# Expert rows scaled at their copy and added into the residual by adding gathers, in a float32 two-block layer on one core

## The chip, the cores and the metric

One Trainium2 chip, one of its cores. The metric is the device time of one execution of the whole program, in microseconds. The kernel before has a median of 2668.73 us over 3 runs (2668.01 to 2673.38). All times below are of one profiled execution of it unless the text says otherwise, counted from the start of its span.

## The reference

The program computes two blocks on 512 tokens of width 1024, in float32. The first block is a retention and pooling mixer, a mixture of experts and a gated side input; the second a state-space mixer, a convolution mixer and two feed-forward layers. The change lies in the mixture of experts and in what follows it directly:

```python
def moe(hn, router_w, router_b, w_gu, b_gu, w_down, b_down):
    logits = xt @ router_w + router_b
    top_vals, top_idx = lax.top_k(logits, TOP_K)        # 4 of 32
    gates = jax.nn.softmax(top_vals, axis=-1)
    ...
    gu = lax.ragged_dot(xs, w_gu, group_sizes) + b_gu[sorted_e]
    act = (up + 1.0) * (gate * jax.nn.sigmoid(SWIGLU_ALPHA * gate))
    y = lax.ragged_dot(act, w_down, group_sizes) + b_down[sorted_e]
    y = y * gates.reshape(-1)[order][:, None]
    return jnp.zeros_like(xt).at[tok].add(y)

h = h + moe(rms_norm(h, norm_moe_w), ...)
gate = jax.nn.sigmoid(rms_norm(h, norm_ple_w) @ ple_gate_w)
h = h + gate * (p @ ple_proj_w)
```

## The kernel before, in words

Every engine has its own program, written out by hand, and semaphores tie them together; there is no scheduler. So the order of an engine's instructions is the order of the code.

**Router (about 260 to 300 us).** VectorE picks four experts per token (`choose`), gives each of the 2048 (token, expert) pairs a tile and a row in it (tiles of 128 rows; expert e owns tile e, further tiles are numbered from 32), and builds one-hot matrices `row_hot` (pair to row) and `tile_token`. TensorE multiplies them (L2374): the product is, per tile, which token stands in each row. VectorE then makes the gates (`gate_table`, L1704), copies the token ids to integers (L1735) and lets GpSimd gather the first tile's tokens (L771). `extra_tables` (L1715) makes the indices by which rows are fetched at the end.

**Experts (300 to 1440 us).** For e = 0 to 31: 8 weight tiles up, 4 down, each split by ScalarE (`slot_hi`, L995) and VectorE (`slot_lo`, L1760) into two parts, for three products on TensorE (L2417). `store_y` (L1017) copies the 128 rows of expert e - 1 or e - 2 from PSUM to `y_sb` and stores them to `y_dram`, unscaled. GpSimd gathers the tokens of the next tile. With the inputs used here no expert has more than 128 tokens, so the code under `If(extra > 0)` is not run.

**Combine (1440 to 1545 us).** After the last store GpSimd issues 16 gathers (`take`, L787), four per group of 128 tokens, into 16 buffers `got`. VectorE adds the down biases, which TensorE has multiplied by the gates (L2504, L1845), and then for each token group i four rows times gate (`combine`, L1853, 16 instructions on L1856). Each group is squared and summed on ScalarE (`moe_square`), its inverse root taken on VectorE (`ple_rstd`), transposed on TensorE (`token_columns`), and multiplied by `ple_w_sb` (`ple_gate`, L2519, two halves per group) whose rows ScalarE has scaled before (L1114). `ple_product` (L2527) is the side input times its weights; `ple_add` on VectorE joins the two. Between these VectorE places steps for the next stage: `c_power` (three instructions, L1849 to L1851) eight times, `turn_angles` and `reduce_turns`. ScalarE's sine block (L1194 on) waits for the last of these, and the second block's first transposes wait for it. SP loads `m_t` for the next stage (8 transfers) once `s_got_used` is 3.

The order of TensorE around the change is:

```python
pe.wait_ge(s_prep_dve, 5)
pe.wait_ge(s_ple_in, 48)
columns_of(p_rows, 2)
...
ple_product(0)
token_columns(0)
for i in range(NT):
    ple_gate(i, 0)
    if i:
        ple_product(i)
    if i + 1 < NT:
        token_columns(i + 1)
    ple_gate(i, 1)
```

## Time and profile before

| | us |
|---|---|
| median of 3 runs | 2668.73 |
| the profiled execution, its own time | 2666.62 |
| its span | 2664.9 |
| TensorE busy (matmul) | 2579.0 |
| VectorE busy | 1947.5 |
| ScalarE busy | 1355.8 |
| GpSimd busy | 198.2 |

The span runs from the first to the last instruction in the trace; the execution's own time has 1.7 us around it. A busy share is an average over stages with different limits, so each stretch has to be read by itself. Rows of the timeline give start, duration, engine, line, operation, output and inputs, and in brackets how long the engine stood idle before and what released it. DMA rows give the time from the issue on the engine's queue to the last byte's semaphore.

### The profile page before, as it was taken

The page shows a single profiled execution, that of the slowest core. Times are in us where ns is not written, and L with a number is a line of the kernel's source. Part 1 is how long each engine was busy: PE and PEld are TensorE (multiplying, and loading weights), DVE is VectorE, ACT ScalarE, POOL GpSimd, SP SyncE. Part 2 cuts the span into 40 slices and gives each one's busy share as a digit, 9 for nine tenths or more (in the row PEclk, how much of TensorE's full clock was granted, in tenths as well). Part 3 has the DMA queues.
Part 4 walks back from the last instruction along what each step waited for, and adds up shares of the span by engine and source line. Part 5 has one row for each costly group of instructions (what it writes and reads, how often), then busy time and mean ns, then how long its engine had stood idle before and what let it go on. Part 6 is the DMA issues. An engine that isn't in the chain of part 4 may idle for free.

```text
span 2664.9 us, 34816 instructions
## 1 busy us (share of the span) xinstructions
PE 2579.0 (97%) x12452; PEld 2113.6 (79%) x12452; DVE 1947.5 (73%) x1892; ACT 1355.8 (51%) x1366; POOL 198.2 (7%) x297
## 2 busy tenths in 40 slices
PE   9999899999999999999998978999999999999998
PEld 7777788888888888888885467888888887888886
DVE  7968899999999999999998986566633444543422
ACT  5232777777777777777775343322222222322222
POOL 2241100000000000000002000011100000000000
PEclk9999999999999999999998998999999999999999
DMA  9734899999999999999996922277643632133432
GB/s 343 280 137 126 356 362 410 384 388 385 387 383 385 390 383 384 387 386 386 385 362 237 161 76 77 59 224 225 188 113 87 156 95 56 48 95 100 108 94 75
DMA packets 351280, 643.89 MB, mean 242 GB/s; under 512 B 27056, under 2 KB 220464, under 8 KB 350192
## 3 DMA queue, kind: packets, MB, share of 16 engines
q1 hardware_dynamic: 327840, 542.88, 59.5%
q0 software_dynamic: 17872, 78.13, 8.3%
q10 hardware_dynamic: 5504, 22.02, 2.0%
q8 instruction: 41, 0.67, 0.1%
q14 instruction: 23, 0.19, 0.0%
HBM read 616.82 MB, written 26.16 MB: 241 GB/s over the span
## 4 chain that ended last, share of the span: by engine, by line
PE 71%; issue 15%; DVE 10%; DMA 2%; ACT 2%; POOL 0%; ACTq 0%; POOLq 0%; DVEq 0%; SPq 0%
PE bank L2417 39%; PE bank L2664 8%; PE bank L2670 8%; PE bank L2665 8%; PE bank L2393 1%; PE bank L2405 1%; DVE cb L1433 1%; PE bank L2400 1%; DMA ring<-in_w_in 1%; PE bank L2227 1%; DVE rows L1856 1%; PE bank L2229 1%; PE bank L2228 1%; DVE ring L2004 0%; DMA m_w_dram<-work 0%
## 5 line engine op out<-in xcount | busy, mean ns | idle before, releaser
L1760 DVE TENSOR_TENSOR slot_lo<-ring,slot_hi 128x2048 fp32r<-128x2048 f32 x384 | 863.7, 2285 | 68.2 <-ACT slot_hi L995 67.8
L995 ACT ACTIVATE slot_hi<-ring 128x2048 fp32r<-128x2048 f32 x384 | 736.5, 1921 | 252.9 <-PE bank L2417 226.6
L2417 PE MATMUL bank<-slot_hi,xs_hi 128*128 128x512 f32 x1024 | 316.8, 391 | 0.0
L2417 PE MATMUL bank<-slot_hi,xs_lo 128*128 128x512 f32 x1024 | 315.7, 389 | 0.0
L2664 PE MATMUL bank<-h_hi,fin_hi 128*128 128x512 f32 x704 | 275.1, 391 | 0.0
L2665 PE MATMUL bank<-h_hi,fin_lo 128*128 128x512 f32 x704 | 274.1, 389 | 0.0
L2417 PE MATMUL bank<-slot_lo,xs_hi 128*128 128x512 f32 x1024 | 274.1, 389 | 0.0
L2417 PEld LDWEIGHTS bank<-slot_hi,xs_lo 128*128 128x128 f32 x1024 | 192.4, 188 | 40.8
L2417 PEld LDWEIGHTS bank<-slot_hi,xs_hi 128*128 128x128 f32 x1024 | 192.5, 188 | 40.2
L2417 PEld LDWEIGHTS bank<-slot_lo,xs_hi 128*128 128x128 f32 x1024 | 192.2, 188 | 40.2
L1255 ACT ACTIVATE fin_hi<-rows 128x1024 fp32r<-128x1024 f32 x88 | 88.2, 1052 | 215.5 <-DMA rows<-in_w_ffn_in 215.5
L2025 DVE TENSOR_TENSOR fin_lo<-rows,fin_hi 128x1024 fp32r<-128x1024 f32 x88 | 103.7, 1221 | 115.2 <-ACT fin_hi L1255 113.1
L2670 PE MATMUL bank<-h_lo,fin_hi 128*128 128x512 f32 x704 | 166.7, 389 | 0.0
L2417 PE MATMUL bank<-slot_hi,act_hi 128*128 128x512 f32 x512 | 161.1, 396 | 2.7 <-DVE act_lo L1769 2.7
L2417 PE MATMUL bank<-slot_hi,act_lo 128*128 128x512 f32 x512 | 158.2, 390 | 0.0
L2664 PEld LDWEIGHTS bank<-h_hi,fin_hi 128*128 128x128 f32 x704 | 132.2, 188 | 28.4 <-issue 1.0
L2670 PEld LDWEIGHTS bank<-h_lo,fin_hi 128*128 128x128 f32 x704 | 132.2, 188 | 27.4
L2665 PEld LDWEIGHTS bank<-h_hi,fin_lo 128*128 128x128 f32 x704 | 132.2, 188 | 27.2
L2417 PE MATMUL bank<-slot_lo,act_hi 128*128 128x512 f32 x512 | 137.7, 391 | 0.0
L2664 PE MATMUL bank<-f_hi,fout_hi 128*128 128x512 f32 x352 | 137.6, 391 | 0.0
L2665 PE MATMUL bank<-f_hi,fout_lo 128*128 128x512 f32 x352 | 137.0, 389 | 0.0
L1300 ACT ACTIVATE ring<-bank 128x512 f32<-128x512 f32 x60 | 35.8, 597 | 195.2 <-PE bank L2670 195.2
(448 smaller groups left out, 4060.0 us busy)
## 6 DMA issues: line engine op xcount, KB each, us to landing
ring<-in_expert_w_gate_up SPq DMA_DIRECT2D x256, 1024.0 KB, 7.1
ring<-in_expert_w_down SPq DMA_DIRECT2D x128, 1024.0 KB, 6.6
rows<-in_w_ffn_in SPq DMA_DIRECT2D x88, 512.0 KB, 4.9
work<-in_w_ada POOLq DMA_DIRECT2D x64, 384.0 KB, 3.8
y_dram<-cb ACTq DMA_DIRECT2D x32, 512.0 KB, 6.9
rows<-in_w_ada POOLq DMA_DIRECT2D x35, 384.0 KB, 5.9
work<-in_w_ffn_out SPq DMA_DIRECT2D x8, 1408.0 KB, 7.0
rows<-in_w_ffn_out SPq DMA_DIRECT2D x8, 1408.0 KB, 6.8
```

Of the source, the lines that this page charges most:

```text
L995: act.activation(hi_of(e, j), slot[q], ACT.Copy).then_inc(s_slot_hi, 1)
L1255: act.activation(split[n][0][b][:, v], raw[:, v], ACT.Copy).then_inc(s_w_hi, 1)
L1300: act.activation(sig_sb[b], ps[3 * b + bank][:], func).then_inc(s_lin_sig, 1)
L1433: return stt(acc, w, cact[:, k:k + 1], acc, ALU.mult, ALU.add)
L1760: tt(slot_lo[:, q], slot[q], whole(hi_of(e, j)), ALU.subtract).then_inc(s_slot_lo, 1)
L1856: ins = stt(rows[:, i, :], got[n], weights[:, n:n + 1], rows[:, i, :], ALU.mult, ALU.add)
L2025: tt(split[n][1][at][:, v], buf[at][:, v], whole(split[n][0][b][:, v]), ALU.subtract).then_inc(s_w_lo, 1)
L2227: mm(ps[i][:], mix_hi[:, k, tokens], w_hi[:, k, :], start=(k == 0), stop=False)
L2417: last = mm(ps[banks + n], x[:, k, :], (lo if lower else hi)[:, k, 512 * n:512 * (n + 1)], start=(begins and lower == 0 and k == 0 and x i ...
L2664: mm(ps[3 * b + v][:], w_hi[b][:, v, k, :], x_hi[:, k, :], start=(k == 0), stop=False)
L2665: mm(ps[3 * b + v][:], lo[:, v, k, :], x_hi[:, k, :], start=False, stop=False)
L2670: last = mm(ps[3 * b + v][:], w_hi[b][:, v, k, :], x_lo[:, k, :], start=False, stop=(k == depth[n] - 1))
```

## The change

1. The gate goes to the row where it is computed. `gate_table` also builds `tile_gate` (one-hot over 48 tiles times gate), 16 small products on TensorE give `slot_gate`, the gate of every row of every tile, and the copy of an expert's rows out of PSUM is scaled by it (`scaled_y`; one more 128x1 copy per tile brings the gate to a fixed place).
2. The 16 gathers add into `rows` in the DMA (`compute_op=ALU.add`). Adds into the same group must follow each other, so each waits for the one before it on that group: groups 0 and 1 alternately, k = 0 to 3, then groups 2 and 3. They start when tile 30 has been stored. VectorE's 16 multiply-adds go.
3. The last expert's rows aren't stored: 8 one-hot products (`last_hot`) add them in PSUM beside the down bias, and `y_dram`'s last tile holds zeros (`zero_rows`). `last_rows` replaces `add_down_bias`.
4. The ids are copied before `gate_table`; `extra_tables` moves between two weight splits of expert 0.
5. The norm weights are applied to `h_cols` (8 copies of 128x128 per group) and no longer to the 16 pieces of `ple_w_sb`.
6. The orders around it: below and in the diff. SP's `m_t` loads no longer wait for `s_got_used` 3.

```diff
+ROW_PAIR = (3, 0, 2, 1)
...
@@ SP
-            sp.wait_ge(s_slot_done, extra * 12 + 12 * E - 4)
+            sp.wait_ge(s_sig_ready, extra * 2 + 2 * E)
...
             sp.wait_ge(s_k_out, 16 * (CH + 1))
-            sp.wait_ge(s_got_used, 3)
@@ GpSimd
+            def add_rows(source, index, i, k, done):
+                n = index + TOPK * i + k
+                pool.indirect_dma_start(
+                    out=rows[:, i, :], out_offset=None, in_=source, compute_op=ALU.add,
+                    in_offset=bass.IndirectOffsetOnAxis(ap=smi[:, n:n + 1].bitcast(U32), axis=0)).then_inc(done, 16)
...
+            pool.wait_ge(s_zero_rows, 16)
+            pool.wait_ge(s_y_stored, 16 * E)
+            for first in (0, 2):
+                for k in range(TOPK):
+                    for i in (first, first + 1):
+                        if k:
+                            pool.wait_ge(s_got_in[i], 16 * k)
+                        add_rows(y_dram, 20, i, k, s_got_in[i])
...
-            take(y_dram, 20, s_got_in)
@@ ScalarE
+            def scaled_y(tile, done, stored, home=y_sb):
+                act.wait_ge(s_slot_gate, 2)
+                act.wait_ge(s_y_sb, tile * 2 + 1)
+                act.activation(gate_col, slot_gate[:, bass.ds(tile, 1)], ACT.Copy).then_inc(s_gate_col, 1)
+                act.wait_ge(s_slot_done, done)
+                act.wait_ge(s_y_stored, stored)
+                act.wait_ge(s_gate_col, tile + 1)
+                for n in range(2):
+                    act.activation(home[:, 512 * n:512 * (n + 1)], ps[4 + n], ACT.Copy, scale=gate_col).then_inc(s_y_sb, 1)
...
+            act.dma_start(zero_rows, whole(pick[:].rearrange("p n t -> p (n t)")).unsqueeze(1).broadcast_to([P, 4, 2 * P])).then_inc(s_zero_rows, 16)
...
-            act.wait_ge(s_ple_in, 48)
-            for n in range(2):
-                for k in range(KD):
-                    act.activation(ple_w_sb[n][:, k, :], ple_w_sb[n][:, k, :], ACT.Copy,
-                                   scale=vcol("norm_ple_w", k)).then_inc(s_prep_act, 1)
@@ VectorE
+                step(tt(tile_gate, iota[:, 0:TILES].unsqueeze(1).broadcast_to(picked),
+                        pick_t.unsqueeze(2).broadcast_to(picked), ALU.is_equal))
+                tt(tile_gate, tile_gate, flat_gates, ALU.mult).then_inc(s_slot_gate, 1)
...
-            def add_down_bias(i):
+            def last_rows(i):
                 dve.wait_ge(s_gates_ps, i + 2)
-                tt(rows[:, i, :], rows[:, i, :], pairs[i][:], ALU.add).then_inc(s_prep_dve, 1)
+                dve.wait_ge(s_got_in[i], 16 * TOPK)
+                tt(rows[:, i, :], rows[:, i, :], pairs[ROW_PAIR[i]][:], ALU.add).then_inc(s_got_used, 1)
...
+            for v in range(2):
                 c_power(v)
+            last_rows(0)
+            last_rows(1)
+            c_power(2)
+            ple_rstd(0, 1)
+            last_rows(2)
+            last_rows(3)
+            ple_rstd(1, 2)
+            ple_rstd(2, 4)
+            c_power(3)
+            c_power(4)
             ple_add(0)
@@ TensorE
+            for n in range(NT * TOPK):
+                last = mm(ps[5][:, 0:TILES], row_hot[:, n, :], tile_gate[:, n, :], start=(n == 0), stop=(n == NT * TOPK - 1))
+            last.then_inc(s_ids_ps, 1)
...
+                    mm(bank, gates_t[n][:, P * i:P * (i + 1)], down_bias[n], start=True, stop=False)
+                    last = mm(bank, last_hot[:, i, :], y_sb[:, 512 * n:512 * (n + 1)], start=False, stop=True)
...
+                if i < 2:
+                    pe.wait_ge(s_got_used, 2 + 2 * i)
...
+                else:
+                    pe.wait_ge(s_side_in, 80)
+                    pe.wait_ge(s_got_used, 3)
```

How the order stands at the three places that matter. First VectorE at the router's end, before (L1707 to L1713 are the gate table, L1735 the ids):

```order
L1707 TENSOR_REDUCE sm<-sm 128x4 [waits norm_in,gate_e,dve_step]
L1708 RECIPROCAL sm<-sm 128x4 [waits dve_step]
L1709 TENSOR_TENSOR sm<-sm 128x16 [waits dve_step]
L1710 TENSOR_TENSOR sm<-sm,work 128x16 [waits dve_step]
L1711 TENSOR_TENSOR sm<-sm 128x16 [waits dve_step]
L1712 TENSOR_TENSOR work<-work,sm 128x512 [waits dve_step]
L1713 TENSOR_REDUCE work<-work 128x128 [waits dve_step]
L1735 CAST smi<-bank 128x48 [waits ids_ps]
```

and now (L1755 the ids, L1733 and L1735 the new `tile_gate`):

```order
L1755 CAST smi<-bank 128x48 [waits ids_ps,dve_step]
L1757 COPY sm<-bank 128x1 [waits dve_step]
L1728 TENSOR_REDUCE sm<-sm 128x4 [waits norm_in,gate_e,dve_step]
L1729 RECIPROCAL sm<-sm 128x4 [waits dve_step]
L1730 TENSOR_TENSOR sm<-sm 128x16 [waits dve_step]
L1733 TENSOR_TENSOR work<-const,work 128x768 [waits k_ps,dve_step]
L1735 TENSOR_TENSOR work<-work,sm 128x768 [waits dve_step]
L1737 TENSOR_TENSOR work<-work,sm 128x512 [waits slot_gate]
L1738 TENSOR_REDUCE work<-work 128x128 [waits dve_step]
```

The ids moved from behind the gate table to its front, past a wait for a DMA (`norm_in`). Second, GpSimd's gathers now (before: 16 without a wait between them but one for `gates_ps` after the eighth):

```order
L788 DMA rows<-y_dram,smi 128x1024 [waits y_stored,zero_rows]
L788 DMA rows<-y_dram,smi 128x1024
L788 DMA rows<-y_dram,smi 128x1024 [waits got_in0]
L788 DMA rows<-y_dram,smi 128x1024 [waits got_in1]
L788 DMA rows<-y_dram,smi 128x1024 [waits got_in0]
L788 DMA rows<-y_dram,smi 128x1024 [waits got_in1]
L788 DMA rows<-y_dram,smi 128x1024 [waits got_in0]
L788 DMA rows<-y_dram,smi 128x1024 [waits got_in1]
L788 DMA rows<-y_dram,smi 128x1024 x2
L788 DMA rows<-y_dram,smi 128x1024 [waits got_in2]
```

Five more rows of this kind, waiting for `got_in3` and `got_in2` in turn, follow. Third, TensorE now, from the last expert on (L2522 and L2523 bias and one-hot products, L2539 `ple_gate`, L2550 `ple_product`):

```order
L2523 MATMUL bank<-cb,work 128x512
L2206 MATMUL bank<-const,rows 128x128 [waits cols_taken,got_used]
L2206 MATMUL bank<-const,rows 128x128 x3
L2206 MATMUL bank<-const,rows 128x128 [waits cols_taken]
L2206 MATMUL bank<-const,rows 128x128 x3
L2539 MATMUL bank<-ring,ca 128x512 [waits got_used,cols_taken]
L2539 MATMUL bank<-ring,ca 128x512 x7
L2550 MATMUL bank<-work,ca 128x512 [waits got_used,side_in]
L2550 MATMUL bank<-work,ca 128x512 x3
L2206 MATMUL bank<-const,rows 128x128 [waits cols_taken,got_used]
```

`ple_product(0)`, which stood before the first `ple_gate` and waited for no gather, stands behind it and waits for `s_got_used` 3, that is for token group 2.

## Rows read from the trace of the kernel before

**Rows 1.** Expert loop: whom ScalarE waited for (us, times, longest)

```profile
ACT slot_hi L995 <- PE bank L2417: 224.3, 308, 1.3
```

**Rows 2.** Timeline of TensorE at the router's end: start, us, engine, line, operation

```profile
281.62 3.91 PE L2374 MATMUL bank<-cb,work 128*128 128x48 f32 x32 [0.67 <-ACT cb L975]
...
290.51 1.13 PE L2383 MATMUL bank<-const 128*128 128x256 f32 x4 [0.69 <-ACT nat L840]
296.99 1.94 PE L2393 MATMUL bank<-const,work 128*128 128x128 f32 x8 [5.35 <-DMA work<-hn_dram,smi]
```

**Rows 3.** Timeline of GpSimd there, the first gather of tokens

```profile
290.10 3.02 POOL L771 DMA_INDIRECT work<-hn_dram,smi  x1 [15.41 <-DVEq L1736]
```

**Rows 4.** Timeline of VectorE at the router's end

```profile
286.81 0.17 DVE L1707 TENSOR_REDUCE sm<-sm 128x4 f32<-128x16 f32 x1 [3.16 <-DMA m_w_dram<-work]
...
289.56 0.20 DVE L1735 CAST smi<-bank 128x48 int32<-128x48 f32 x1
```

**Rows 5.** Chain of waits that ended last, 1440 to 1545: start, us, what

```profile
1441.21 6.50 DMA y_dram<-cb
...
1465.49 1.29 DVE rows L1856
```

**Rows 6.** Timeline of TensorE after the last expert

```profile
1456.20 5.21 PE L2527 MATMUL bank<-work,ca 128*128 128x512 f32 x8 [0.78 <-ACT ca L840]
...
1467.23 9.94 PE L2519 MATMUL bank<-ring,ca 128*128 128x512 f32 x16 [1.18 <-ACT ca L840]
1477.01 1.04 PE L2197 MATMUL bank<-const,rows 128*128 128x128 f32 x8
1477.89 13.90 PE L2519 MATMUL bank<-ring,ca 128*128 128x512 f32 x32
1491.62 3.60 PE L2527 MATMUL bank<-work,ca 128*128 128x512 f32 x8
```

**Rows 7.** Timeline of VectorE, 1480 to 1525

```profile
1480.67 1.22 DVE L1849 TENSOR_TENSOR ring<-work,cb 128x1024 f32<-128x1024 f32 x1
...
1484.44 0.69 DVE L1876 TENSOR_TENSOR cb<-cb,bank 128x512 f32<-128x512 f32 x1
...
1487.10 5.24 DVE L1856 SCALAR_TENSOR_TENSOR rows<-nat,sm,rows 128x1024 f32<-128x1024 f32 x4
1493.55 0.17 DVE L1372 TENSOR_SCALAR sm<-sm 128x2 f32<-128x2 f32 x1 [1.22 <-ACT cb L845]
...
1496.11 1.22 DVE L1881 TENSOR_TENSOR nat<-rows,ca 128x1024 f32<-128x1024 f32 x1 [0.23 <-DVE sm L1367]
...
1508.72 0.38 DVE L1907 COPY sm<-par 64x32 f32<-64x32 f32 x2
...
1523.57 0.69 DVE L1876 TENSOR_TENSOR nat<-nat,bank 128x512 f32<-128x512 f32 x1 [0.22 <-DVE work L1382]
```

**Rows 8.** Timeline of ScalarE, 1424 to 1500

```profile
1424.89 0.35 ACTq L1023 DMA_DIRECT2D y_dram<-cb  x1
...
1443.95 9.91 ACT L1114 ACTIVATE ring<-ring,vec 128x512 f32<-128x512 f32 x16 [2.77 <-DMA ring<-in_ple_gate_w]
...
1484.96 0.69 ACT L1139 ACTIVATE cb<-bank,sm 128x512 f32<-128x512 f32 x1 [5.05 <-PE bank L2519]
1492.37 1.06 ACT L845 ACTIVATE cb<-rows 128x1024 f32<-128x1024 f32 x1 [6.73 <-DVE rows L1856]
```

**Rows 9.** Timeline of GpSimd: one of the sixteen issues

```profile
1452.25 0.94 POOL L791 DMA_INDIRECT ring<-y_dram,smi  x1 [0.30 <-issue]
```

**Rows 10.** Issue to landing: GpSimd's gathers of expert rows, L791

```profile
DMA to landing us min/median/max: 5.3/6.0/7.6
```

**Rows 11.** Issue to landing: GpSimd's gathers of tokens in the loop, L762

```profile
DMA to landing us min/median/max: 5.0/5.9/8.8
```

**Rows 12.** Stretches: us, busy PE, PEld, DVE, ACT, POOL, PEclk, DMA share, GB/s

```profile
1440.00:1444.00 4.00, 0.98 (x3) 0.50 (x4) 3.90 (x4) 1.13 (x3) 0.00 (x0) 0.78 1.05 400
1444.00:1448.00 4.00, 4.00 (x12) 1.69 (x10) 3.90 (x4) 4.00 (x7) 0.13 (x1) 0.50 0.51 203
```

More of the change, by code:

```diff
@@ L393, in program @@
         s_y_stored = sem("y_stored")
-        s_more_zero = sem("more_zero")
+        s_zero_rows = sem("zero_rows")
+        s_slot_gate = sem("slot_gate")
+        s_gate_col = sem("gate_col")
         s_ct_ps = sem("ct_ps")
@@ L784, in _ @@
                     next_tile(n + E)
-            def take(source, index, done):
-                for n in range(NT * TOPK):
-                    if n == 2 * TOPK:
-                        pool.wait_ge(s_gates_ps, NT + 1)
-                    pool.indirect_dma_start(
-                        out=got[n], out_offset=None, in_=source,
-                        in_offset=bass.IndirectOffsetOnAxis(ap=smi[:, index + n:index + n + 1].bitcast(U32), axis=0),
-                    ).then_inc(done[n // TOPK], 16)
-            pool.wait_ge(s_y_stored, extra * 16 + 16 * (E + 1))
-            pool.wait_ge(s_xst_ready, extra * 2 + 2 * E + 2)
-            pool.tensor_tensor(smi[:, 130:131], smi[:, 52:53], smi[:, 52:53], ALU.add)
-            with pool.If(extra > 0):
-                take(y_more, 36, [s_more_in] * NT)
-                pool.wait_ge(s_more_used, NT)
-            take(y_dram, 20, s_got_in)
+                pool.wait_ge(s_y_stored, extra * 16 + 16 * E)
+                pool.tensor_tensor(smi[:, 130:131], smi[:, 52:53], smi[:, 52:53], ALU.add)
+                for i in range(NT):
+                    pool.wait_ge(s_got_in[i], 16 * TOPK)
+                for k in range(TOPK):
+                    for i in range(NT):
+                        if k or i:
+                            pool.wait_ge(s_more_in, 16 * (NT * k + i))
+                        add_rows(y_more, 36, i, k, s_more_in)
             def token_rstd(n):
@@ L1131, in token_columns @@
                 for r in range(2):
-                    column(h_cols[i % 2][:, 512 * r:512 * (r + 1)], first=6)
+                    n = rounds[0]
+                    rounds[0] += 1
+                    act.wait_ge(s_cols_ready, n + 1)
+                    for k in range(4 * r, 4 * r + 4):
+                        part = act.activation(h_cols[i % 2][:, P * k:P * (k + 1)], ps[6 + n % 2][:, P * (k % 4):P * (k % 4 + 1)],
+                                              ACT.Copy, scale=vcol("norm_ple_w", k))
+                    part.then_inc(s_cols_taken, 1)
             def ple_gate(i, n):
@@ L1698, in _ @@
             step(dve.tensor_copy(smi[:, 52:56], token))
-            step(ts(ext_e, pick_t, float(E), None, ALU.is_ge))
-            more, main = sm[:, 176:192], sm[:, 160:176]
             gate_rows = work[:, 8192:8192 + NT * E].rearrange("p (i e) -> p i e", i=NT)
@@ L1797, in _ @@
             split_low(0, 0)
-            extra_tables()
             tokens_low(0)
@@ L1802, in _ @@
                 split_low(0, j)
+                if j == 3:
+                    dve.wait_ge(s_ids_ps, 2)
+                    dve.tensor_copy(slot_gate, ps[5][:, 0:TILES]).then_inc(s_slot_gate, 1)
+                    extra_tables()
             swiglu(0, 0)
@@ L1824, in _ @@
                 low_ahead(E, j)
+            for i in range(NT):
+                step(ts(last_hot[:, i, :], iota, float(P * i), last_token, ALU.add, ALU.is_equal))
+            dve.sem_inc(s_prep_dve, 1)
             n0 = step.n
@@ L1851, in c_power @@
                 step(tt(m_c[:, :, v, :], m_c[:, :, v, :], s5_tb, ALU.add))
-            def combine(i, weights, done):
-                for k in range(TOPK):
-                    n = TOPK * i + k
-                    ins = stt(rows[:, i, :], got[n], weights[:, n:n + 1], rows[:, i, :], ALU.mult, ALU.add)
-                    if k < TOPK - 1:
-                        step(ins)
-                    else:
-                        ins.then_inc(done, 1)
-            def combine_main(i):
-                dve.wait_ge(s_got_in[i], 16 * TOPK)
-                combine(i, main, s_got_used)
             def ple_rstd(first, end):
```

118 lines of the change are left out of this document (48 added, 70 removed).

## The prediction

> **What bounds the kernel now.** I read the chain of waits first, then each engine's timeline in the two stretches that the change touches, then the landing times of the gathers. The expert loop (300 to 1440 us) is TensorE's: the split and the copies wait for it, ScalarE alone 224.3 us in 308 waits [rows 1]. So the change can gain or lose only at the router's end and between the last expert and the second block.
>
> At the router's end TensorE stands still for 5.35 us until the first gather of tokens lands at 296.99 [rows 2]. That gather is issued at 290.10 [rows 3], when VectorE has copied the ids at 289.56, behind a gate table that could begin only at 286.81 because of a DMA [rows 4]. The ids' product was done at 281.62 + 3.91 = 285.5 [rows 2].
>
> After the last expert the chain goes through the last store (6.50 us), the gathers, and then VectorE's multiply-adds [rows 5]. The reader is to see that from 1477.9 on TensorE and VectorE are both nearly full: TensorE's first product behind group 0, `ple_product(1)`, starts at 1491.62 without a gap [rows 6], and VectorE reaches `ple_add(2)`, which lets the sine block begin, at 1523.57 with 0.22 us idle [rows 7]. Whoever is late sets the end, and both hang on `ple_add(0)`.
>
> **The sum, part by part.**
>
> *Ids first.* They are copied at about 285.7 instead of 289.56, and the gather, whose issue to landing is 296.99 - 290.10 = 6.9 us, issued at about 286.1, lands at 293.0. But TensorE now first does 16 small products for `slot_gate`, of the same shape as the ids' (3.91 us). They wait for VectorE: 286.81, three small steps (0.6), two 768-wide steps of about 1.0 each (the 512-wide part of the gate table took less): 289.6. TensorE is free at 290.5, since the two keep-warm products of 1.13 us go [rows 2]. So it reaches the tokens at 290.5 + 3.9 = 294.4 instead of 296.99: **-2.6 us**. Bounds: 0, if the longer table is late, and -4.0, if only the gather counted. `extra_tables` (2.6 us now) goes between two splits of expert 0; this costs nothing as long as VectorE is ahead of TensorE there. The zero store is issued on ScalarE's queue before the tokens arrive and is waited for ten microseconds later.
>
> *In the loop.* Each tile gets one 128x1 copy on ScalarE, at most 0.3 us, and it stands ahead of the wait for the products. ScalarE waits 224.3 us for TensorE in the loop [rows 1], 32 copies are some 10: **0**. If that cover went, 10 us is the price.
>
> *Start of the adding gathers.* Tile 30's store is issued at 1424.89 [rows 8]; with the 6.50 of the last one [rows 5] it has landed at 1431.4, against 1447.9 before. GpSimd has nothing else then. That is 16 us earlier, and it is what the change is paid with.
>
> *Their length.* The old 16 were issued every 0.94 + 0.30 = 1.25 us [rows 9] and overlapped. Now each waits for the one before on its group. Issue to landing was 6.0 (5.3 to 7.6) [rows 10] and 5.9 (5.0 to 8.8) beside the weights' loads [rows 11]. An add must read the row as well as the source; 0.5 MB at 400 GB/s [rows 12] is 1.3 us, so I take 7.3 per round. No row shows an adding DMA: the ends are 5.0, the shortest plain one, and 8.8 + 1.3 = 10.1. Groups 0 and 1 alternate; group 2 begins two issues behind their fourth round. Group 2 has landed at 1431.4 + 7 x 7.3 + 2.5 = 1485.0, and `last_rows(2)` (1.2) ends at **1486.2**. Under the Trainium skill, page "Collectives: The Full Stack", section "The bandwidth ceiling: the fold count and why AG ≠ RS ≠ AR", a DMA that adds costs twice the source reads and nothing for the sum itself. By that rule the round would be about the same 7.3, and no run here shows it yet.
>
> *TensorE up to there.* The gate weights land at 1443.95 [rows 8], say 1446 with gathers beside them. Then the side input's columns (2.0, twice the 0.9 of eight transposes at full clock [rows 6]), 16 products of 128x512 (0.86 each at full clock from 13.9 / 16 [rows 6], 13.7 in all; 17 taken, because the granted clock is 0.50, 1.2 of 2.4 GHz, behind the pause at 1440 [rows 12]), transposes (1.0), eight copies on ScalarE (2), `ple_gate(0, 0)` (7.3): 1475.3. Bounds 1468.8 (all at full clock) and 1486. There it waits for 1486.2, because `ple_product(0)` needs group 2. **TensorE stands still for 11 us.**
>
> *From there to `ple_add(0)`.* Behind a pause the clock is halved: `ple_product` took 5.2 then and 3.6 later, `ple_gate` 9.94 against 6.9 [rows 6]. So 5.2 + 1.0 + 8.0 (clock back on the way) = 14.2 until `ple_gate(0, 1)` ends. ScalarE squares group 3 only behind that half's sigmoid: 0.7 + 1.2 [rows 8]. VectorE's order puts `ple_rstd(2, 4)` (2.6) and two `c_power` (3.8 each) before `ple_add(0)` (2.7) [rows 7]: 0.7 + 1.2 + 2.6 + 7.6 + 2.7 = 14.8 us, in which TensorE has only 7 us of work. `ple_add(0)` ends at 1486.2 + 14.2 + 14.8 = **1515.2**.
>
> *From `ple_add(0)` on* the order is the old one: `z_rows` 1.2, three `c_power` 11.3, `ple_add(1)` 2.7, `z_rows` 1.2, `turn_angles` and `reduce_turns` 1523.57 - 1508.72 = 14.9 [rows 7], together 31.3. To meet the old 1523.57 `ple_add(0)` would have to end at 1492.3; TensorE's own 1491.62 says the same. It ends **22.9 us later**. The 16 multiply-adds that VectorE sheds (4 x 5.24 = 21 us [rows 7]) turn into waiting, since VectorE stands at `last_rows(2)` and at `ple_rstd(2, 4)`. The 16 weight scalings (9.9 us [rows 8]) and the 13.7 us of new products also lie inside the wait.
>
> Sum: 22.9 - 2.6 = +20.3. The profiled execution's own time is 2666.6, so 2686.9; against the median of the runs, 2668.7, it is **2689 us**.
>
> **The rivals.**
>
> *B, gathers hidden behind TensorE.* If group 2 has landed by 1475 (a round under 5.8 us), TensorE doesn't pause: 1475.3 + 3.4 + 0.9 + 6.9 + 14.8 = 1501.3, +9.0 - 2.6 = +6.4: 2675. For it: 5.9 and 6.0 are medians under load. Against: the add reads more. By the Trainium skill, page "DMA: Bandwidth & Descriptors", section "Anatomy of one DMA — SWDGE (gpsimd) path", one such DMA takes 2.0 us plus its bytes at 436 GB/s, an estimate of 3.2 for 0.5 MB; by that rule B would hold. The trace disagrees: none of the 48 gathers took under 5.0.
>
> *C, gathers slowed by what they run beside.* Rounds of 10.1: group 2 at 1431.4 + 70.7 + 2.5 + 1.2 = 1505.8, `ple_add(0)` 1534.8, +39.9: 2709. For it: the gate weights load until 1444, and SP's eight `m_t` loads now start when group 1 is done, beside the gathers of groups 2 and 3. Against: beside the weights' loads the median stayed 5.9.
>
> *D, the other side: VectorE was the bound, and its 21 us come back.* The chain before does run through the multiply-adds. If gathers land by 1462 (a round under 3.9) and the square of group 3 doesn't hold VectorE, only TensorE's work is left: 1443.95 + 2.0 + 13.7 + 0.9 + 1.3 = 1461.9, then 6.9 + 3.4 + 0.9 + 13.8 = 1486.9 for `ple_product(1)` against 1491.6: -4.7 - 2.6 = -7.3: 2661. It decides once no gather is waited for. Against: eight dependent rounds can't fit, and the written order holds VectorE.
>
> *E, it cancels.* Gathers as in B and TensorE at its lower bound of 1468.8: 1468.8 + 11.2 + 14.8 = 1494.8, +2.5 - 2.6 = 0: 2669, also what a saving that nobody waits for would give.
>
> **How the numbers follow.** Forecast (serial gathers, a pause of TensorE) 0.48; B 0.17; C 0.16; D 0.09; E 0.10. A measurement of this kernel tells 0.2%, 5.3 us, from no change. Slower is forecast, B and C: 0.81; same E: 0.10; faster D: 0.09. The range leaves out D, half of E and the top of C (rounds above 10.7): 2668 to 2714. The forecast's own range, rounds of 6.5 to 8.3, is 2683 to 2696.
>
> **What would show it.** The first add issued near 1429 (the front gain shifts all by 2.6), rounds of about 7 us, in pairs; TensorE idle for some 10 us before `ple_product(0)` and for 5 to 8 before `ple_product(1)`, its granted clock at 0.5 behind each; VectorE idle before `last_rows(2)` and `ple_rstd(2, 4)`; TensorE's tokens at 294.4. I am wrong if adds overlap, if `ple_add(0)` ends before 1495, or if the front idle stays at 5 us.

## The result and the profile after

| | before | after |
|---|---|---|
| median of the runs, us | 2669.54 (2667.69 to 2673.38, 6 runs) | 2723.4 (2716.16 to 2730.3, 6 runs) |
| profiled execution, us | 2666.62 (span 2664.9) | 2725.22 (span 2723.5) |
| TensorE busy, us | 2579.0 | 2612.1 |
| VectorE busy, us | 1947.5 | 1928.5 |
| GpSimd busy, us | 198.2 | 208.1 |

The ratio is 1.0199, 95% interval 1.0186 to 1.0212: 2.0% slower, 53.9 us. I forecast 2689, slower, with a range of 2668 to 2714. The direction was right. The forecast loss, 20.3 us, was less than half of the measured one, and the time lies outside the range. Below, a token tile is the same as a token group: 128 of the 512 tokens.

In this execution the ids' product starts at 284.79 instead of 281.62, ahead of everything that the change touches. Why was not traced; in the profiled executions of the other runs it starts between 1.5 us earlier and 4.0 us later than before. So some 3 us of every shift below are not the change's, and starts of two runs can be compared only to a few us.

TensorE, timeline of after, the first product that each stretch waits for (columns: start and length in us, engine, line, operation, out<-in, shape, count, idle before it and what ended the idle time):

```profile
293.59 4.27 PE L2390 MATMUL bank<-work 128*128 128x48 f32 x32 [0.69 <-ACT nat L850]
297.66 1.93 PE L2405 MATMUL bank<-const,work 128*128 128x128 f32 x8
...
329.69 0.72 PE L2417 MATMUL bank<-bias_parts,pick 128*128 128x512 f32 x2 [3.65 <-DVE xs_lo L1799]
...
1453.25 1.97 PE L2206 MATMUL bank<-const,work 128*128 128x128 f32 x8 [10.39 <-DMA ring<-in_ple_gate_w]
1455.15 2.07 PE L2522 MATMUL bank<-work 32*128 32x512 f32 x2
1457.15 2.07 PE L2523 MATMUL bank<-cb,work 128*128 128x512 f32 x2
...
1490.36 7.13 PE L2539 MATMUL bank<-ring,ca 128*128 128x512 f32 x16 [1.82 <-ACT ca L1153]
1521.05 5.87 PE L2550 MATMUL bank<-work,ca 128*128 128x512 f32 x8 [23.56 <-DVE rows L1876]
...
1549.30 5.42 PE L2550 MATMUL bank<-work,ca 128*128 128x512 f32 x8 [7.77 <-DVE rows L1895]
```

The row at 1549.30 is `ple_product(1)`, which before started at 1491.62 [rows 6]: 57.7 us later, as the whole span is 58.6 longer. So the loss is whole by then, and nothing behind it adds. It is set by the gathers of tile 2, for which TensorE waits 23.56 us ahead of `ple_product(0)`, and by the 28.3 us from there to `ple_product(1)`, 7.77 of them a second wait. TensorE's own work ended at 1497.5. That lies inside the gathers' time here, but late: the sixteen row products (bias and one-hot) took 2.0 us each, so a shorter wait would soon have met them.

GpSimd, timeline of after, the sixteen adding gathers (the idle time before a row is the wait for the one before on the same tile):

```profile
1436.88 1.70 POOL L788 DMA_INDIRECT rows<-y_dram,smi  x1 [52.70 <-DMA y_dram<-cb]
1438.88 1.87 POOL L788 DMA_INDIRECT rows<-y_dram,smi  x1 [0.30 <-issue]
1447.16 2.49 POOL L788 DMA_INDIRECT rows<-y_dram,smi  x1 [6.41 <-DMA rows<-y_dram,smi]
...
1457.45 1.54 POOL L788 DMA_INDIRECT rows<-y_dram,smi  x1 [5.54 <-DMA rows<-y_dram,smi]
...
1464.34 1.56 POOL L788 DMA_INDIRECT rows<-y_dram,smi  x1 [1.87 <-DMA rows<-y_dram,smi]
...
1469.35 1.55 POOL L788 DMA_INDIRECT rows<-y_dram,smi  x1 [0.30 <-issue]
...
1476.22 2.40 POOL L788 DMA_INDIRECT rows<-y_dram,smi  x1 [3.46 <-DMA rows<-y_dram,smi]
...
1491.75 1.55 POOL L788 DMA_INDIRECT rows<-y_dram,smi  x1 [9.14 <-DMA rows<-y_dram,smi]
...
1505.25 1.55 POOL L788 DMA_INDIRECT rows<-y_dram,smi  x1 [8.34 <-DMA rows<-y_dram,smi]
```

Tile 0 issues at 1436.88, 1447.16, 1457.45 and 1464.34: rounds of 10.3, 10.3 and 6.9. Tile 2 issues at 1469.35, 1476.22, 1491.75 and 1505.25: 6.9, 15.5, 13.5. What changes between a round of 6.9 and the others stands on SyncE's queue (the eight loads together, from the start of the first issue to the end of the last), and what it costs on VectorE:

```profile
1475.22 46.23 SPq L527 DMA_DIRECT2D ring<-k_dram  x8
```

```profile
1470.68 1.22 DVE L1876 TENSOR_TENSOR rows<-rows,bank 128x1024 f32<-128x1024 f32 x1 [21.20 <-DMA rows<-y_dram,smi]
1473.58 1.22 DVE L1876 TENSOR_TENSOR rows<-rows,bank 128x1024 f32<-128x1024 f32 x1 [1.69 <-DMA rows<-y_dram,smi]
1519.69 1.22 DVE L1876 TENSOR_TENSOR rows<-rows,bank 128x1024 f32<-128x1024 f32 x1 [38.92 <-DMA rows<-y_dram,smi]
```

The `m_t` loads (`ring<-k_dram`) start at 1475.22, as soon as `last_rows(1)` lets them, and from then on the rounds are twice as long. In the kernel before they started at 1478.41, when the last gather had been issued 7.9 us before, at 1470.54. The first two rounds of tile 0 run beside the gate weights, which were issued 4.2 us later than before and land at 1453.25 instead of 1443.95 [rows 8].

### The profile page after: what moved, and what is told of

Its sections match the earlier page's. It is cut to its first block, busy times and chain, and to the rows that moved or that the text cites. A ratio compares the mean times of both kernels' runs of the same rounds, so it can differ in the third digit from the quotient of the medians.

```text
span 2723.5 us, 35024 instructions
## 1 busy us (share of the span) xinstructions
PE 2612.1 (96%) x12496; PEld 2126.4 (78%) x12496; DVE 1928.5 (71%) x1878; ACT 1359.1 (50%) x1406; POOL 208.1 (8%) x297
## 4 chain that ended last, share of the span: by engine, by line
PE 68%; issue 15%; DVE 10%; DMA 5%; ACT 2%; POOL 0%; SPq 0%; ACTq 0%; DVEq 0%; POOLq 0%
PE bank L2429 37%; PE bank L2684 7%; PE bank L2678 7%; PE bank L2679 7%; DMA rows<-y_dram,smi 3%; PE bank L2405 1%; DVE cb L1456 1%; PE bank L2417 1%; PE bank L2412 1%; DMA ring<-in_w_in 1%; DVE slot_lo L1783 1%; PE bank L2236 1%; PE bank L2237 1%; PE bank L2238 1%; DMA rows<-in_w_ffn_in 1%
## 5 line engine op out<-in xcount | busy, mean ns | idle before, releaser
L1005 ACT ACTIVATE slot_hi<-ring 128x2048 fp32r<-128x2048 f32 x384 | 733.0, 1918 | 245.1 <-PE bank L2429 218.9
```

The costliest lines, as they stand in the source:

```text
L1005: act.activation(hi_of(e, j), slot[q], ACT.Copy).then_inc(s_slot_hi, 1)
```

## The experiments

Two theories stood at first. **M**: the `m_t` loads, no longer held by `s_got_used` 3, slow the gathers of tiles 2 and 3. **A**: the adding itself is slow. Later runs took apart what stood behind each bound that a run removed. Unless said otherwise a start is that of the profiled execution.

### 1. The m_t loads behind the gathers

```diff
             sp.wait_ge(s_k_out, 16 * (CH + 1))
+            sp.wait_ge(s_got_used, NT)
             for v in range(CH):
                 load(m_t[...], ..., s_t_in)
```

> The changed kernel, but SP's eight m_t loads wait for all four token groups (s_got_used 4). Theory M: these loads stretch the adding rounds of groups 2 and 3 from 6.9 us (the two rounds at 1457 and 1469, with nothing beside them) to 13.5 to 15.5. Then the rounds go back to about 7, group 2 lands at 1469.4 + 4 x 7 = 1497 instead of 1519.6, and the time is about 2701. Rival N: two adding gathers in flight are slow of themselves; then nothing changes, 2723.

Measured: 2703.06 (2701.48 to 2704.25), ratio 1.0124 (1.0105 to 1.0142), so 20.3 us come back. TensorE's timeline of this kernel:

```profile
1453.12 1.97 PE L2207 MATMUL bank<-const,work 128*128 128x128 f32 x8 [11.83 <-DMA ring<-in_ple_gate_w]
...
1490.26 8.96 PE L2540 MATMUL bank<-ring,ca 128*128 128x512 f32 x16 [1.41 <-ACT ca L1154]
1499.06 3.60 PE L2551 MATMUL bank<-work,ca 128*128 128x512 f32 x8
...
1525.03 5.21 PE L2551 MATMUL bank<-work,ca 128*128 128x512 f32 x8 [7.77 <-DVE rows L1896]
```

and VectorE's:

```profile
1493.27 1.22 DVE L1877 TENSOR_TENSOR rows<-rows,bank 128x1024 f32<-128x1024 f32 x1 [14.94 <-DMA rows<-y_dram,smi]
```

Tile 2 lands at 1493.3 instead of 1519.7, its rounds are 7.6, 7.6 and 6.6, and TensorE no longer waits ahead of `ple_product(0)`: its own work, which reaches it at 1499.06, has become the bound. M holds and is worth 20 us. The gathers by themselves would have let it start at 1494.5, so this bound lies only 4.6 us behind theirs. The loads' own lateness costs nothing: `m_t` is read only behind the x columns, the first of which start at 1573.75 in this kernel.

### 2. Gathers that copy instead of add

```diff
-                    out=rows[:, i, :], out_offset=None, in_=source, compute_op=ALU.add,
+                    out=rows[:, i, :], out_offset=None, in_=source,
```

This leaves out the adding: of each token only the last gathered row remains, without the residual. The chain of waits is that of after.

> The changed kernel, its 16 gathers with the same waits, but copying instead of adding, so that the rows before and three of four expert rows are lost. If the add itself is what costs (issue 1.55 against 0.94 us, landing 10.2 against 6.0), rounds fall to about 6.2 and the time to about 2690. If it is what they run beside, landing stays near 9 and the time above 2710.

Measured: 2704.76, one run. Issue 0.94 us each instead of 1.55; from issue to landing 4.3, median 8.2, up to 15.1 (after: 6.0, 10.2, 15.1). Tile 2 lands at 1502.6 instead of 1519.7. A round without loads beside it took 5.7 (1462.97 to 1468.67) against 6.9 with adds. Beside the gate weights the rounds of tile 0 were 8.0 and 9.0 against 10.3 and 10.3. Beside `m_t` those of tile 2 were 15.4 and 13.1, as with adds (15.5, 13.5 and 14.4). So both theories hold a part: the adding costs 1.2 us in a round by itself and 1.3 to 2.3 beside the gate weights, and beside `m_t` the form of the gather makes no difference that one execution can show. With one run, the 18.6 us by which it is faster than the change are no more than a sign.

### 3. Four tiles abreast

```diff
-            for first in (0, 2):
-                for k in range(TOPK):
-                    for i in (first, first + 1):
+            for k in range(TOPK):
+                for i in range(NT):
```

on top of run 1.

> e1, and k is the outer loop with all four groups inside: four dependent rounds instead of eight. Theory (latency of dependent rounds): four issues of 1.85 us fill a round, rounds of 8 to 10, all groups landed by about 1475, TensorE no longer waits for group 2 but is bound by its row products until 1487; ple_product(1) at about 1524 instead of 1549, so about 2697. Rival (the DMA engines' rate for adds is the limit, abreast doesn't help): as e1, 2701 or more.

Measured: 2707.75 (2704.74 to 2711.13), ratio 1.0136 (1.0116 to 1.0156). A miss: nothing was gained. TensorE shows why:

```profile
1460.80 1.97 PE L2206 MATMUL bank<-const,work 128*128 128x128 f32 x8 [19.79 <-DMA ring<-in_ple_gate_w]
...
1506.33 3.60 PE L2550 MATMUL bank<-work,ca 128*128 128x512 f32 x8
```

The last gather was issued at 1477.6 instead of 1489.3, but landings rose to 9.6 to 13.9 us, and the gate weights, in the same DMA engines, landed 8 us later still. Everything of TensorE's stands behind them, so what the gathers gained was lost there. The rival, that the DMA engines' rate is the limit, holds in part. Two windows in which adding gathers are all that moves, run 1 (two tiles in turn) first and this kernel second; the last two columns are the DMA engines' busy share and GB/s:

```profile
1485.00:1495.00 10.00, 8.59 (x18) 4.40 (x18) 1.22 (x1) 3.21 (x10) 3.10 (x2) 0.55 0.97 170
```

```profile
1475.00:1485.00 10.00, 10.00 (x11) 2.48 (x11) 3.77 (x4) 1.15 (x2) 3.10 (x2) 0.50 1.06 211
```

Two adding gathers in flight already keep the engines at 0.97, and four bring 211 GB/s instead of 170. So more gathers abreast hide little of the 6.9 us of a round: twice as many in flight bring a quarter more, and each lands later for it (median 11.6 us instead of 6.8).

### 4. The ids first, in the kernel before

```diff
-            gate_table()
-
             dve.wait_ge(s_ids_ps, 1)
             step(dve.tensor_copy(smi[:, 80:80 + TILES], ps[6][:, 0:TILES]))
             dve.sem_inc(s_route_ok, 1)
+            gate_table()
```

> The kernel before, with only the copy of the ids moved ahead of the gate table. The gather of the first tokens is issued about 4 us earlier; TensorE's idle 5.35 us shrink to between 1.3 and 2.7, so -2.6 to -4 us, 2666.5. Rival: VectorE, which the early start finds still at its tables, gives it back in expert 0; 2669.5.

Measured: 2668.35 (12 runs) against 2669.83 (17 runs), ratio 0.999 (0.9982 to 0.9999): 1.5 us by the medians, and between 0.3 and 4.8 by the interval. The gather is issued at 287.98 and TensorE's 5.35 us of idle are gone, but the next bound is 2 us behind: `xs_lo` stands behind `extra_tables` on VectorE.

### 5. Row products ahead of the gate weights

```diff
-            pe.wait_ge(s_ple_in, 48)
-            for k in range(2):
-                column([p_rows[...] for i in range(NT)], first=2)
             pe.wait_ge(s_bias_in, 32)
...
             for i in range(NT):
                 if i == 3:
+                    pe.wait_ge(s_ple_in, 48)
+                    for k in range(2):
+                        column([p_rows[...] for r in range(NT)], first=2)
                     pe.wait_ge(s_cols_taken, COLS_P)
```

on top of run 1.

> e1_mt_late with the row products of the first three token tiles moved ahead of TensorE's wait for the ple_gate weights (the fourth stays behind the p columns). Theory (the 32 us of products stand behind the weights, and the next bound is the gathers): products start near 1446 instead of 1455; at 2.0 us each the sixteen with the p columns end near 1480 instead of 1487; ple_product(0) then waits for last_rows(2), whose gathers landed at 1493.3 in e1_mt_late, so it starts near 1495 instead of 1499.1: about 4 us gained, 2699. If the half clock came from the 10 us of idle ahead of the products, they now run at the full clock, 1.0 us each, and end near 1463; the time is the same 2699, since the gathers bound it. Rival (the weights' landing is what bounds the time by another way, through ple_gate(0,0)): no gain, 2703.

Measured: 2703.75 (2700.31 to 2705.34), ratio 1.0122 (1.0106 to 1.0137): no gain. The products did move, and they did not get faster. TensorE's timeline:

```profile
1445.01 1.16 PE L2523 MATMUL bank<-work 32*128 32x512 f32 x2 [1.36 <-ACT cb L1036]
1446.09 2.08 PE L2524 MATMUL bank<-cb,work 128*128 128x512 f32 x2
...
1466.12 2.08 PE L2524 MATMUL bank<-cb,work 128*128 128x512 f32 x2
...
1470.59 1.12 PE L2523 MATMUL bank<-work 32*128 32x512 f32 x2 [0.69 <-ACT ca L851]
1471.64 1.12 PE L2524 MATMUL bank<-cb,work 128*128 128x512 f32 x2
...
1499.05 6.12 PE L2551 MATMUL bank<-work,ca 128*128 128x512 f32 x8 [10.51 <-DVE rows L1877]
```

Two things. The pause ahead of them was now 1.36 us, yet from the second to the twelfth product each took 2.0 us at a granted clock of 0.50: the products stay at half clock without the pause of 10 us, to which I had put it down. And TensorE, ready earlier, now waits 10.51 us for tile 2, whose gathers land at 1497.7 here (they began 2.4 us later in this execution); behind that pause `ple_product(0)` takes 6.12 us instead of 3.60. The two bounds of run 1 were a few us apart, so taking one away gave nothing. My 4 us were the distance between them without the price of the new pause.

### 6. The two kinds of product apart

```diff
                 for i in tiles:
                     for n in range(2):
                         mm(pairs[ROW_PAIR[i]][:, 512 * n:512 * (n + 1)], gates_t[n][:, P * i:P * (i + 1)], down_bias[n], start=True, stop=False)
+                for i in tiles:
+                    for n in range(2):
                         last = mm(pairs[ROW_PAIR[i]][:, 512 * n:512 * (n + 1)], last_hot[:, i, :], y_sb[:, 512 * n:512 * (n + 1)], start=False, stop=True)
```

on top of run 5; `tiles` is (0, 1, 2), then (3).

> e5_rows_first with the six 32-row bias products first and then the six one-hot ones, instead of alternately (then two and two). Theory (the turns between the two forms cost the time: each product waits 1.5 us ahead of its weight load): the 32-row ones take 0.9 us each, as before's eight took 7.20 us, and TensorE is done some 9 us sooner than in e5_rows_first. Rival (the half clock alone makes the 2.0 us): each still 2.0 us, the same end. The time is that of e5_rows_first in both cases, since the gathers bound it.

Measured: 2702.36, one run. TensorE's timeline:

```profile
1443.57 2.84 PE L2523 MATMUL bank<-work 32*128 32x512 f32 x12 [1.36 <-ACT cb L1036]
1446.34 5.42 PE L2526 MATMUL bank<-cb,work 128*128 128x512 f32 x12
1453.22 1.09 PE L2207 MATMUL bank<-const,work 128*128 128x128 f32 x8 [1.46 <-DMA ring<-in_ple_gate_w]
1455.05 2.08 PE L2523 MATMUL bank<-work 32*128 32x512 f32 x4 [0.74 <-ACT ca L851]
1457.06 3.78 PE L2526 MATMUL bank<-cb,work 128*128 128x512 f32 x4
```

and the windows 1440 to 1445, 1445 to 1450 and 1455 to 1460 (the column PEclk is the granted clock):

```profile
1440.00:1445.00 5.00, 3.64 (x18) 2.22 (x18) 4.86 (x5) 1.26 (x2) 0.55 (x1) 1.00 1.06 247
1445.00:1450.00 5.00, 5.00 (x17) 2.09 (x14) 2.18 (x2) 0.00 (x0) 2.64 (x2) 1.00 1.05 339
...
1455.00:1460.00 5.00, 4.95 (x8) 1.68 (x8) 0.00 (x0) 0.33 (x2) 2.31 (x2) 0.50 0.94 178
```

The same products at the same place: a 32-row one 2.84 / 6 = 0.47 us and a one-hot one 5.42 / 6 = 0.90, at a granted clock of 1.00 (2.4 GHz), instead of 2.0 each at 0.50 (1.2 GHz). In turns at the full clock, as in the rows at 1470.59 and 1471.64 of run 5, each took 1.05; so the turns double the time of the 32-row product and add a sixth to the one-hot one, and the clock doubles both. The last four products, here at 0.50, took 1.04 and 1.89. All sixteen: 14.1 us instead of 32. It is one execution, but runs 9 to 12 keep this order and show the same 2.84 and 5.42 us for the first twelve. The time is the same as in run 5, as both theories had it: TensorE now waits 7.81 us for tile 0 and 16.20 us for tile 2.

### 7. ple_add(0) ahead of ple_rstd(2, 4)

```diff
-            ple_rstd(2, 4)
             c_power(3)
             c_power(4)
             ple_add(0)
+            ple_rstd(2, 4)
```

on top of run 1.

> e1_mt_late with VectorE's ple_rstd(2,4), which waits for ScalarE's last square, moved behind c_power(3), c_power(4) and ple_add(0). Theory (the pause of 7.77 us ahead of ple_product(1) is VectorE's order alone): the pause goes, ple_product(1) starts near 1517.5 instead of 1525.0, time 2695. Rival (ScalarE's gate behind ple_rstd(2,4) is late in its place): the pause comes back ahead of a later gate, 2703.

Measured: 2697.01 (2694.08 to 2699.33), ratio 1.0099 (1.0083 to 1.0114): 6 us, and the pause of 7.77 us is gone:

```profile
1504.02 13.90 PE L2540 MATMUL bank<-ring,ca 128*128 128x512 f32 x32
1517.76 3.60 PE L2551 MATMUL bank<-work,ca 128*128 128x512 f32 x8
```

### 8. The ids first and the tables later, in the kernel before

```diff
             split_low(0, 0)
-            extra_tables()
             tokens_low(0)
...
             tokens_low(1)
+            extra_tables()
             split_low(1, 2)
```

on top of run 4.

> e4_ids_first (the kernel before with the ids copied ahead of the gate table) and, beside it, the tables for extra tiles moved from ahead of the first xs_lo to behind those of expert 1. Theory: in e4_ids_first the first expert product waited 2.13 us for xs_lo, which stood behind those tables, so it starts near 296.3 instead of 298.4 and the gain stays: 2666 against 2669.5. Rival (VectorE's splits of expert 0 are the bound, and what is gained at the front is waited for at expert 1's xs_lo): 2668, as e4_ids_first.

Measured: 2668.52 (11 runs) against 2670.69 (15 runs), ratio 0.9996 (0.9987 to 1.0005). The first product did start at 295.46, but at 335.94 TensorE waits 2.55 us for the activations of expert 0 (`DVE work`), behind the tables in their new place. The rival's time is the one measured, and the wait came back as it says, though in expert 0 and not at expert 1's `xs_lo` (1.21 us there, as before): VectorE isn't ahead in these two experts, and moving its 2.6 us of tables gained nothing.

### 9. The parts together, and the last tile's products late

Runs 1, 6 and 7 together, and:

```diff
-ROW_PAIR = (3, 0, 2, 1)
+ROW_PAIR = (3, 2, 1, 1)
...
-        gate_sb = [cb[:, 0:1024]] + [nat3[:, i, :] for i in range(1, NT)]
+        gate_sb = [work[:, 4096:5120]] + [nat3[:, i, :] for i in range(1, NT)]
...
+            row_products(range(3))
             pe.wait_ge(s_ple_in, 48)
...
-                    pe.wait_ge(s_got_used, 3)
+                    pe.wait_ge(s_got_used, 2)
...
                 ple_gate(i, 1)
+                if i == 0:
+                    pe.wait_ge(s_got_used, 3)
+                    row_products((3,))
```

On VectorE `ple_rstd(1, 2)`, `c_power(3)` and `c_power(4)` stand ahead of `last_rows(2)`.

> The parts that the runs so far point to, together: m_t behind the gathers (e1_mt_late), the 32-row products apart from the one-hot ones and ahead of the gate weights (e6_bias_apart), ple_add(0) ahead of ple_rstd(2,4) (e7_add_first); and the pairs of banks given out so that ple_product(0) waits for two token tiles instead of three, with the products of the last tile behind ple_gate(0,1). Theory (what bounds e7_add_first is the adding gathers of tiles 2 and 3, waited for ahead of ple_product(0)): ple_product(0) starts near 1481 instead of 1499.6, TensorE then waits only ahead of the last tile's products and of ple_gate(1,0), ple_product(1) starts near 1509 instead of 1517.8: 2689. Rival (the gathers' end near 1497 to 1502 sets the time whatever stands behind it): no more than 3 us gained on e7_add_first's 2697.

Measured: 2691.79 (2688.27 to 2694.28), ratio 1.0085 (1.0069 to 1.01). `ple_product(0)` starts at 1482.49, `ple_product(1)` at 1507.59; what is left in between are waits of 2.37 us (tile 2) and 1.41 us. The longest wait now stands ahead of both, for the four gathers of tile 0:

```profile
1469.24 1.97 PE L2207 MATMUL bank<-const,rows 128*128 128x128 f32 x8 [14.32 <-DVE rows L1877]
```

So the row products, done early, are no longer the bound, and the gathers are again.

### 10. The tables later

```diff
                     dve.tensor_copy(slot_gate, ps[5][:, 0:TILES]).then_inc(s_slot_gate, 1)
-                    extra_tables()
...
             tokens_low(1)
+            extra_tables()
             split_low(1, 2)
```

on top of run 9.

> e9_third_late and, beside it, the tables for extra tiles moved from the middle of expert 0's splits on VectorE to behind the xs_lo of expert 1. Theory (VectorE isn't ahead in expert 0, and the tables' 2.6 us are what TensorE waits for at expert 1's xs_lo): that idle of 3.6 us falls to about 1.2 and the time by 2.4: 2686.5. Rival (it is given back further on in expert 1, as most of the gain in e8_ids_tables_late seems to be): 2689.

Measured: 2691.37 (2688.21 to 2698.64), ratio 1.0089 (1.0072 to 1.0105): nothing. TensorE's idle at expert 1's `xs_lo` falls from 3.65 to 1.77 us, and 14 us further on stands a wait that run 9 didn't have:

```profile
326.89 0.73 PE L2418 MATMUL bank<-bias_parts,pick 128*128 128x512 f32 x2 [1.77 <-DVE xs_lo L1800]
340.97 0.66 PE L2413 MATMUL bank<-const,work 128*128 128x128 f32 x4 [1.99 <-DVE work L1778]
```

### 11. Twelve copies and four adds

```diff
-            for first in (0, 2):
-                for k in range(TOPK):
-                    for i in (first, first + 1):
-                        if k:
-                            pool.wait_ge(s_got_in[i], 16 * k)
-                        add_rows(y_dram, 20, i, k, s_got_in[i])
+            for i in range(NT):
+                add_rows(y_dram, 20, i, 0, s_got_in[i])
...
+            pool.wait_ge(s_y_sb, extra * 2 + 2 * E + 1)
...
+            for i in range(NT):
+                for k in range(1, TOPK):
+                    n = 20 + TOPK * i + k
+                    pool.indirect_dma_start(
+                        out=got[3 * i + k - 1], out_offset=None, in_=y_dram,
+                        in_offset=bass.IndirectOffsetOnAxis(ap=smi[:, n:n + 1].bitcast(U32), axis=0)).then_inc(s_got_in[i], 16)
...
+                for k in range(1, TOPK):
+                    step(tt(rows[:, i, :], rows[:, i, :], got[3 * i + k - 1], ALU.add))
```

on top of run 10. `got` is eight buffers of the weight ring and four of `nat`, free once the last expert's products are done.

> e10_tables_late with only the first gather of each token tile adding into the residual, and the other twelve plain copies into twelve buffers (free once the last expert's products are done), added by VectorE, three more adds of 1.22 us for each tile. Theory (the adding in the DMA engines is what costs: 56 to 61 us for sixteen gathers at 150 to 190 GB/s with the DMA engines busy, against 300 to 400 GB/s for the copies before): the twelve are issued in 15 us behind 1444, the last lands near 1466, last_rows(3) is done near 1475 instead of 1500, TensorE hardly waits behind ple_product(0), and ple_product(1) starts near 1493: 2671. Rival (the bytes bound both forms alike, or VectorE's twelve adds do): last_rows(3) near 1490 or later, 2681 or more.

Measured: 2691.03 (2684.48 to 2694.71), ratio 1.0081 (1.0067 to 1.0095): a miss, the time of run 10. But the transfers did what the theory says. Windows 1455 to 1465 and 1475 to 1485, run 9 (adds) first and this kernel (copies) second; the last two columns are the DMA engines' busy share and GB/s:

```profile
1455.00:1465.00 10.00, 0.00 (x0) 0.00 (x0) 0.00 (x0) 0.94 (x4) 4.52 (x4) 0.65 0.98 169
...
1475.00:1485.00 10.00, 10.00 (x20) 4.20 (x19) 8.80 (x29) 0.69 (x1) 5.09 (x4) 0.83 0.93 183
```

```profile
1455.00:1465.00 10.00, 1.97 (x8) 1.57 (x8) 4.53 (x4) 1.54 (x4) 2.29 (x3) 0.50 1.03 412
...
1475.00:1485.00 10.00, 10.00 (x31) 4.86 (x30) 8.97 (x24) 2.87 (x9) 0.00 (x0) 1.00 0.01 2
```

With the DMA engines equally full, copies moved 412 GB/s and adds 169, and all rows had landed before 1475 instead of at about 1497. Tile 0's rows, though, came late: VectorE began to add them at 1460.37, so `ple_gate(0, 0)` started only 3.8 us sooner than in run 9. From there the order ate the gain: `last_rows(2)` stood until 1486.38 behind three powers, and the last tile's products until 1491.43 behind it and `ple_gate(0, 1)`. `ple_product(1)` started at 1509.48, 1.9 us later than in run 9, though this execution's last expert product had ended 3.4 us sooner.

### 12. The same with another order

```diff
-            c_power(2)
+            last_rows(2)
             ple_rstd(0, 1)
             ple_rstd(1, 2)
-            c_power(3)
-            c_power(4)
-            last_rows(2)
+            c_power(2)
             last_rows(3)
+            c_power(3)
             ple_add(0)
+            c_power(4)
...
-                ple_gate(i, 1)
                 if i == 0:
                     pe.wait_ge(s_got_used, 3)
                     row_products((3,))
+                ple_gate(i, 1)
```

> e11_copies with last_rows(2) ahead of ple_rstd(0,1) and of c_power(2) to (4) on VectorE, last_rows(3) ahead of c_power(3), and TensorE's products for the last tile ahead of ple_gate(0,1). Theory (in e11_copies the last gathers landed by 1475, but last_rows(2) stood until 1486.4 behind the powers and the last tile's products until 1491.4 behind ple_gate(0,1), so what was left was order and not transfers): last_rows(2) ends near 1475, last_rows(3) near 1491 instead of 1499.5, ple_gate(1,0) isn't waited for, ple_product(1) starts near 1500.5 instead of 1509.5: 2682. Rival (the powers moved back now delay ple_add(0) and with it ple_product(1)): 2688 or more.

Measured: 2685.27 (2678.19 to 2690.32), ratio 1.0058 (1.0045 to 1.0072), against 2723.4 for the change. `ple_product(1)` started at 1496.38 without a wait:

```profile
1482.65 13.90 PE L2550 MATMUL bank<-ring,ca 128*128 128x512 f32 x32
1496.38 3.60 PE L2561 MATMUL bank<-work,ca 128*128 128x512 f32 x8
```

It is still 0.6% slower than the kernel before, which reaches the same product 4.8 us earlier [rows 6], and 8.3 us sooner if both are counted from the end of the last expert's products (1440.1 before, 1436.6 in this execution, the shortest of the six). And the kernel before issues its first gather of expert rows at 1448.82, this one at 1429.64. Here the gate weights still land at about 1450 beside gathers, and tile 0's four rows are together only at 1457. No run separates what is left into the one-hot products, the order and the transfers. None of the versions with the adding gathers or their copies beat the kernel before. Run 4, which has neither, is 0.1% below it, and run 8's 0.04% can't be told from nothing.

## Why the prediction was wrong in size

**The step that failed is "Their length": 7.3 us a round.** A round by itself was 6.9, in runs 1 and 9 6.6 to 7.7, so the figure was right for adding gathers without a load beside them. Beside the gate weights it was 10.3, beside `m_t` 15.5, 13.5 and 14.4 (to the landing). The seven rounds of the sum and the step from group 0 to group 2 took 1519.7 - 1436.9 = 82.8 us where I had 7 x 7.3 + 2.5 = 53.6. The excess of 29.2 us is 21.5 beside `m_t`, 6.0 beside the gate weights and 2.5 in the step (5.0 instead of 2.5), less 0.8 in the two other rounds. Without the step a round was 11.1 on average, above the upper end of 10.1, which came from plain gathers. `ple_product(0)` began at 1521.05 where I had 1486.2, 34.85 us later: 29.2 from the rounds and 5.5 from their later start, 3.2 of which are this execution's front. `ple_product(1)` was later than forecast by the same 34.8 (57.7 against 22.9), so nothing was lost between the two.

**Rival C, which names both the gate weights and the `m_t` loads, was the right mechanism, and I argued it away** with the plain gathers' median of 5.9 beside the weights [rows 11]. Those gathers fetched tokens one at a time in the loop; that row said nothing of two at a time, adding, beside large loads. That the engines were full there was on record: a share of 1.05 at 1440 to 1444 [rows 12]. C's time, 2709, was 14 us too low: its seven rounds and the step come to 73.2 us instead of 82.8, and its gathers start 5.5 us early. The 3.2 us for 0.5 MB by the rule quoted there (the Trainium skill, page "DMA: Bandwidth & Descriptors", section "Anatomy of one DMA — SWDGE (gpsimd) path") don't agree with run 2 either, whose shortest plain gather took 4.3 us. Rival B, which hung on such short rounds, did not come.

**"Start of the adding gathers"**: 1436.88 instead of 1431.4. Tile 30's store was issued at 1429.30, 4.4 us later than before, 3.2 of them the front of this execution, and took 7.6 us instead of 6.5.

**"TensorE up to there"**: 1475.3 taken, 1497.5 measured. The weights landed at 1453 instead of 1446, the products took 32 us instead of 17. Eight of the sixteen were not new either: the kernel before has its eight bias products (L2504, 7.20 us). In the change all this is hidden behind the wait for tile 2. Run 1 shows that it becomes the bound when the wait goes: its `ple_product(0)` starts at 1499.06, 12.9 us behind the forecast, which is most of the 14 us that run 1 is slower than 2689. Runs 5 and 6 show that the pause, to which the sum put the half clock down, isn't needed for it: two kinds of product in turns are enough. So a second term of the sum was mis-sized, and it was luck that the change itself doesn't show it.

**"From there to `ple_add(0)`" and on**: right. From `ple_product(0)` to `ple_product(1)` 28.3 us, taken 29.0; the waits fell where the prediction put them, with a low granted clock behind each (0.55 and 0.62 over the next 5 us), and run 7 shows that the second is VectorE's order.

**"Ids first"**: tokens 2.5 us sooner relative to the ids' product, taken 2.6. The condition in "this costs nothing as long as VectorE is ahead" doesn't hold. TensorE's idle at expert 1's `xs_lo` went from 1.21 to 3.65 us, and the last expert ends, counted from the ids' product, as late as before within 0.4 us. So of the -2.6 in the sum nothing is left at the end of the loop. Runs 8 and 10 show that the tables' place doesn't matter.

**"In the loop: 0"** holds: ScalarE still waits for TensorE there (218.9 us in all), and the end of the loop didn't move.

**The rule on adding transfers** (the Trainium skill, page "Collectives: The Full Stack", section "The bandwidth ceiling: the fold count and why AG ≠ RS ≠ AR": twice the reads, nothing for the sum): by itself a round is 6.9 against 5.7, which it allows. At a share of 0.98 the engines moved 169 GB/s with adds, at 1.03 they moved 412 with copies, a factor of 2.3 in engine time per byte as the profile counts them. In run 2 two copies in flight moved 217 GB/s at a share of 0.64 (1462 to 1470), two adds in run 1 170 at 0.97: a factor of 1.9. The rule's doubling lies between the two.

## What to carry to other kernels

A chain of dependent transfers is priced by what shares the DMA engines with it at that hour, not by its own latency: look for every load whose release the change touches, and keep large loads behind the chain if nobody reads them soon. Letting the DMA engines add took 19 us of work from VectorE (1947.5 to 1928.5), which only waited instead, and gave it to engines that were full. And before paying for one bound to go, find the distance to the next: runs 3, 5, 10 and 11 each shortened the wait that they were meant to shorten and gained nothing.

## What was not expected of the hardware

- Sixteen fp32 products of 512 columns, 32-row and 128-row ones in turns, held TensorE at a granted clock of 0.50 for 32 us without a gap (2.0 us each); the first twelve of them in two blocks ran at 1.00 (0.47 and 0.90 us), behind the same pause of 1.36 us at which, in turns, the clock fell within two products. Why the turns keep the clock down is open; no run tells weight loads from row groups.
- An adding gather keeps GpSimd 1.55 us for the issue, a copying one 0.94, for the same 128 rows of 4 KB.
- The first gather's issue took 3.02 us in the kernel before and 1.05 us in run 4, where it is issued 2 us sooner. The first adding gather's took 3.72, 3.69 and 3.40 us in runs 5, 7 and 12, and 1.6 to 1.9 in the others. This wasn't followed up.
